# Sample attention woven into prompt attention, ahead of the delta rule

## The reference

```
n = RMSNorm(x);  [A | B] = n @ w_in
h = x + w_out @ concat(A, B);   y = h + PEER(RMSNorm(h))
A: softmax attention, 8 heads x 64, dilated windows (128,1), (512,4), (2048,16)
   sample: 4 queries x 8 heads against 2048 cached keys/values per sequence
B: gated delta rule, 4 heads, key and value width 128
PEER: 16384 single-neuron experts, 8 product-key heads, top 16
outputs: y_prompt, y_sample, K/V windows, conv and delta states of both groups
```

## Time and profile before

| | us |
|---|---|
| median of 3 runs (lowest, highest) | 2330.55 (2328.76, 2334.92) |
| the profiled execution's time | 2327.75 |
| its span, first to last instruction | 2325.8 |
| PE busy | 2071.7 (89%) |
| DVE busy | 1576.0 (68%) |
| POOL busy | 1153.3 (50%) |
| ACT busy | 775.6 (33%) |
| mean granted clock of PE, share of full speed | 0.938 |

### The profile page before, as it was taken

The page is one execution under the profiler, slowest core; times in us unless marked ns, Lnnn a source line. Parts: engine busy times, 40 slices in busy tenths (PEclk is TensorE's granted clock), DMA queues, the critical chain, the costliest instruction groups (busy, mean ns, idle before and its releaser), DMA issues.

```text
span 2325.8 us, 34649 instructions
## 1 busy us (share of the span) xinstructions
PE 2071.7 (89%) x12706; PEld 1919.7 (83%) x12706; DVE 1576.0 (68%) x3094; ACT 775.6 (33%) x1230; POOL 1153.3 (50%) x632
## 2 busy tenths in 40 slices
PE   5999998787567898999999788889989999999998
PEld 5989756675346898999888788879979999999998
DVE  2378434433332301879986999994369999999996
ACT  3223233222232322444444434333323333333332
POOL 2326002131001231566676344337778888888884
PEclk9999758896798899999999999999989999999999
DMA  6453245542874121467777667678978989899894
GB/s 220 145 176 115 73 192 215 217 152 79 277 253 137 53 88 60 140 213 239 227 237 243 223 241 273 231 279 340 355 281 313 331 310 317 309 314 315 316 324 138
DMA packets 176596, 520.94 MB, mean 224 GB/s; under 512 B 15152, under 2 KB 86064, under 8 KB 170704
## 3 DMA queue, kind: packets, MB, share of 16 engines
q1 hardware_dynamic: 136560, 290.94, 36.2%
q0 software_dynamic: 36864, 134.23, 17.2%
q10 hardware_dynamic: 3056, 94.24, 10.3%
HBM read 456.81 MB, written 128.49 MB: 252 GB/s over the span
## 4 chain that ended last, share of the span: by engine, by line
PE 42%; DVE 40%; issue 6%; ACT 4%; POOL 3%; DMA 3%; SPq 2%; ACTq 0%; DVEq 0%; PEldq 0%
DVE acc_g L1850 10%; DVE act_l L1834 9%; PE bank L2210 7%; PE bank L2211 6%; PE bank L2212 6%; DVE one L1529 6%; DVE one L1528 5%; DVE rows_g L1698 3%; PE twin L2210 3%; PE twin L2212 3%; PE twin L2211 3%; POOL u_lo L1673 2%; PE bank L464 1%; DMA ks<-kc 1%; PE bank L646 1%
## 5 line engine op out<-in xcount | busy, mean ns | idle before, releaser
L1673 POOL TENSOR_TENSOR u_lo<-u_raw,u_hi 128x1024 fp32r<-128x1024 f32 x128 | 315.9, 2468 | 330.1 <-ACT u_hi L1653 329.4
L2210 PE MATMUL bank<-hn_hi,u_hi 128*128 128x416 f32 x1024 | 373.8, 365 | 33.9 <-POOL u_lo L1673 33.6
L1878 POOL TENSOR_TENSOR v_lo<-v_raw,v_hi 128x1024 fp32r<-128x1024 f32 x128 | 336.0, 2626 | 70.4 <-ACT v_hi L1803 69.2
L2211 PE MATMUL bank<-hn_lo,u_hi 128*128 128x416 f32 x1024 | 363.6, 355 | 0.0
L2212 PE MATMUL bank<-hn_hi,u_lo 128*128 128x416 f32 x1024 | 362.0, 354 | 0.0
L1850 DVE SCALAR_TENSOR_TENSOR acc_g<-rows_g,coef,acc_g 128x1024 f32<-128x1024 f32 x127 | 289.3, 2278 | 18.0 <-DMA rows_g<-ev,idx_g 17.6
L2211 PE MATMUL bank<-a_lo,v_hi 128*128 128x416 f32 x768 | 269.4, 351 | 0.0
L2210 PE MATMUL bank<-a_hi,v_hi 128*128 128x416 f32 x768 | 269.2, 351 | 0.0
L2212 PE MATMUL bank<-a_hi,v_lo 128*128 128x416 f32 x768 | 269.1, 350 | 0.0
L2210 PEld LDWEIGHTS bank<-hn_hi,u_hi 128*128 128x128 f32 x1024 | 195.9, 191 | 49.2 <-POOL u_lo L1673 47.1
L1834 DVE TENSOR_TENSOR act_l<-act_l,gin 128x416 f32<-128x416 f32 x128 | 229.6, 1794 | 0.0
(11 more groups left out here) (436 smaller groups left out, 4740.8 us busy)
## 6 DMA issues: line engine op xcount, KB each, us to landing
u_raw<-eu SPq DMA_DIRECT2D x128, 512.0 KB, 4.9
v_raw<-ev SPq DMA_DIRECT2D x128, 512.0 KB, 4.7
k_s<-kc ACTq DMA_DIRECT2D x29, 1104.0 KB
v_s<-vc ACTq DMA_DIRECT2D x29, 1104.0 KB
acts_dram<-act_c SPq DMA_DIRECT2D x128, 208.0 KB, 3.8
gates_dram<-gst ACTq DMA_DIRECT2D x8, 3328.0 KB, 12.5
gin<-gates_dram SPq DMA_DIRECT2D x32, 832.0 KB, 7.9
act_l<-acts_dram SPq DMA_DIRECT2D x64, 416.0 KB, 5.6
```

Source lines behind the costliest of these rows:

```text
L1673: nc.gpsimd.tensor_tensor(out=u_lo[s][:], in0=u_raw[2 * (x % 2) + s][:], in1=u_hi[s][:].bitcast(F32), op=ALU.subtract).then_inc(dn["ulo"], 1)
L1878: nc.gpsimd.tensor_tensor(out=v_lo[f % 4][:], in0=v_raw[f % 4][:], in1=v_hi[f % 4][:].bitcast(F32), op=ALU.subtract).then_inc(dn["vlo"], 1)
L2210: nc.tensor.matmul(out, ah, bh, start=first and i == 0, stop=False)
L2211: nc.tensor.matmul(out, ah, bl, start=False, stop=False)
```

## The change

The sample stage is dissolved into prompt attention. Each sample batch has four consecutive slots (`SLOTS_B`), one prompt unit each. PE turns key pairs 0 and 1 around unit 0, pairs 2 and 3 around unit 1, turns the previous batch's probabilities ahead of unit 2 and computes the batch's scores after it, and multiplies the previous batch's values ahead of unit 3. The PSUM banks are shared: prompt scores have two banks and run two units ahead, turned prompt probabilities one bank, prompt values one, and the sample work the other four. K, V, `kt_lo`, `kt_hi` and `qbd` go to the space of the projection's input and weights, which is free when the last projection product is out, and SP issues their first loads then. The queries' block matrix `qbd` is written by DVE ahead of the first scores. The delta rule starts when both attentions are done. The delta states are loaded after the last values; the first w_out slice has a buffer of its own (`w_first`) and is loaded then too. Its split by ACT comes after the delta rule's last copy, and POOL's low halves wait for the store of the sample states, whose space `w_lo` shares. The copies of the cache are 10 pairs in the projection (slices 2 to 11), none in attention, 12 in the delta rule, 8 in the query products.

The diff, cut to its core:

```diff
         ks = [put(f"ks{s}", [P, KTILES, AH * AD]) for s in range(2)]
-        vs_old = [None, put("vs_old1", [P, OLD_TILES, AH * AD])]
-        assert put.pos[0] <= R_W
-        put = region(R_AQ)
-        vs_old[0] = put("vs_old0", [P, OLD_TILES, AH * AD])
-        vs_new = [put(f"vs_new{s}", [P, NEW_TILES, AH * AD]) for s in range(2)]
-        assert put.pos[0] <= R_AV
-        kt_lo = at("kt_lo", R_BZ, [P, PAIRS, KT_SPLIT])
-        put = region(R_E)
+        vs = [put(f"vs{s}", [P, KTILES, AH * AD]) for s in range(2)]
+        kt_lo = put("kt_lo", [P, PAIRS, KT_SPLIT])
+        kt_hi = put("kt_hi", [P, PAIRS, CACHED - KT_SPLIT])
+        qbd = put("qbd", [P, NB, PAIRS, QROWS])
+        assert put.pos[0] <= R_AQ
+        put = region(R_E + 8192 + 4096)
         sss = [put(f"sss{s}", [P, CACHED + QROWS]) for s in range(2)]
         pts = put("pts", [P, KTILES + 1, QROWS])
-        qbd = put("qbd", [P, NB, PAIRS, QROWS])
-        kt_hi = put("kt_hi", [P, PAIRS, CACHED - KT_SPLIT])
+        put = region(R_STAT + 160)
         ob = put("ob", [P, P])
         seat_t = put("seat_t", [P, P + PAIRS * NL])
         own_half, fold = seat_t[:, 0:P], seat_t[:, P:]
+        assert put.pos[0] <= R_STAT + 160 + NT * 64 + 3 * CH * 32
+        w_first = at("w_first", R_E, [P, CH, WC])
...
-        COPIES_W, COPIES_A, COPIES_D = NW1 // 2, -(-SEQ // P * AH // 3), 2 * (LEVELS - 1)
-        COPIES = COPIES_W + COPIES_A + COPIES_D
+        COPIES_W, COPIES_D, COPIES_F = 10, 2 * (LEVELS - 1), 8
+        COPIES = COPIES_W + COPIES_D + COPIES_F
...
+        TURN_LO, TURN_HI, SCORE_LO, SCORE_HI = 4, 5, 6, 7
+        value_out = bank[TURN_LO][:, 0:P]
+        folded = bank[SCORE_LO][:, 0:PAIRS * NL]
...
+        def sp_attend(sp):
+            sp.wait_ge(proj_ready, READY1)
+            sp.wait_ge(w_lo_ready, NW1)
+            for b in range(2):
+                load_cached(sp, b, kc)
+            sp.wait_ge(rope_done, NT)
+            sp.dma_start(seat_t[:], lnc_s[:, CACHED + NB * QROWS:]).then_inc(small_in, 16)
+            for b in range(2):
+                load_cached(sp, b, vc)
+            for b in range(2, NB + 1):
+                if b < NB:
+                    sp.wait_ge(sa["kt0"], PAIRS * (b - 1))
+                    sp.wait_ge(sa["kt1"], PAIRS * (b - 1))
+                    load_cached(sp, b, kc)
+                if b > 2:
+                    sp.wait_ge(sa["used"], b - 2)
+                    load_cached(sp, b - 1, vc)
+            sp.wait_ge(sa["used"], NB)
+            sp.wait_ge(s_cat, len(UNITS) // 2)
+            sp.dma_start(w_first[:], wout[0]).then_inc(w_in[0], 16)
+            sp.dma_start(w_raw[1][:], wout[1]).then_inc(w_in[1], 16)
...
             def scores(u):
                 i, h = UNITS[u]
-                if u >= 4:
-                    pe.wait_ge(s_masked, u - 3)
+                if u >= 2:
+                    pe.wait_ge(s_masked, u - 1)
                 r = slice(AD * (h % 2), AD * (h % 2) + AD)
-                nc.tensor.matmul(bank[2 + u % 4][:, 0:(i + 1) * P], qkt[r, h // 2, i * P:(i + 1) * P],
+                nc.tensor.matmul(bank[2 + u % 2][:, 0:(i + 1) * P], qkt[r, h // 2, i * P:(i + 1) * P],
                                  qkt[r, PAIRS + h // 2, 0:(i + 1) * P], start=True, stop=True).then_inc(s_scores, 1)
 
             def turn(u):
                 i, h = UNITS[u]
                 pe.wait_ge(s_norm, u + 1)
-                if u >= 2:
-                    pe.wait_ge(s_pt, u - 1)
+                if u:
+                    pe.wait_ge(s_pt, u)
                 for j in range(i + 1):
-                    last = nc.tensor.transpose(quad(u % 2)[:, j, :], sm[:, u % 4, j * P:(j + 1) * P], ident)
+                    last = nc.tensor.transpose(quad(0)[:, j, :], sm[:, u % 4, j * P:(j + 1) * P], ident)
                 last.then_inc(s_turned, 1)
...
+            def turn_keys(b, p):
+                s, q = b % 2, b * PAIRS + p
+                if p == 0:
+                    pe.wait_ge(keys_in[s], 16 * 4 * (b // 2 + 1))
+                    if b >= 2:
+                        pe.wait_ge(s_kept, KEPT0 + b - 1)
+                if q:
+                    pe.wait_ge(sa["kta"], q)
...
+            def sample_scores(b):
+                pe.wait_ge(sa["kta"], PAIRS * (b + 1))
+                pe.wait_ge(sa["ktv"], PAIRS * (b + 1))
+                if b:
+                    pe.wait_ge(sa["masked"], b)
+                if b >= 2:
+                    pe.wait_ge(sa["os"], b - 1)
...
+            def turn_sample(b):
+                s = b % 2
+                pe.wait_ge(sa["norm"], b + 1)
+                keys_turned = PAIRS * min(b + 2, NB)
+                pe.wait_ge(sa["kta"], keys_turned)
+                pe.wait_ge(sa["ktv"], keys_turned)
+                if b == NB - 1:
+                    pe.wait_ge(s_kept, KEPT0 + b)
...
+            def fold_heads(b):
+                pe.wait_ge(small_in, 16 * 10)
+                pe.wait_ge(s_kept, KEPT0 + b + 1)
+                pe.wait_ge(sa["masked"], min(b + 2, NB))
+                if b == NB - 1:
+                    pe.wait_ge(sa["os"], b)
+                nc.tensor.matmul(folded, ob[:], fold, start=True, stop=True).then_inc(s_fold, 1)
+
+            pe.wait_ge(sa["q"], 1)
+            scores(0)
+            scores(1)
             for u in range(len(UNITS)):
+                b, k = divmod(u, SLOTS_B)
+                if k == 0:
+                    if b >= 2:
+                        fold_heads(b - 2)
+                    turn_keys(b, 0)
+                elif k == 1:
+                    turn_keys(b, 2)
+                elif k == 2 and b:
+                    turn_sample(b - 1)
+                elif k == 3 and b:
+                    sample_values(b - 1)
                 turn(u)
                 if u:
                     values(u - 1)
-                if u + 4 < len(UNITS):
-                    scores(u + 4)
+                if u + 2 < len(UNITS):
+                    scores(u + 2)
+                if k == 0:
+                    turn_keys(b, 1)
+                elif k == 1:
+                    turn_keys(b, 3)
+                elif k == 2:
+                    sample_scores(b)
             values(len(UNITS) - 1)
+            fold_heads(NB - 2)
+            turn_sample(NB - 1)
+            sample_values(NB - 1)
+            fold_heads(NB - 1)
...
+            dve.wait_ge(proj_ready, READY1)
+            chain.link(nc.vector.memset(qbd[:], 0.0))
+            for h in range(AH):
+                r = slice(AD * (h % 2), AD * (h % 2) + AD)
+                chain.mark(nc.vector.tensor_copy(qbd[r, :, h // 2, (h % 2) * NL:(h % 2 + 1) * NL],
+                                                 qkt[r, h // 2, SEQ:TOK].rearrange("p (b l) -> p b l", b=NB)))
+            chain.join()
+            dve.sem_inc(sa["q"], 1)
...
             mask(0)
-            mask(1)
             for u in range(len(UNITS)):
-                if u + 2 < len(UNITS):
-                    mask(u + 2)
+                b, k = divmod(u, SLOTS_B)
+                if k in (1, 2):
+                    keys(b, 2 * k - 1)
+                if u + 1 < len(UNITS):
+                    mask(u + 1)
+                if k in (0, 1):
+                    keys(b, 2 * k)
                 n = (UNITS[u][0] + 1) * P
                 dve.wait_ge(s_exp, u + 1)
                 chain.link(nc.vector.reciprocal(smax[:, u % 4, 3:4], smax[:, u % 4, 2:3]))
                 nc.vector.tensor_scalar(sm[:, u % 4, 0:n], sm[:, u % 4, 0:n], smax[:, u % 4, 3:4], None, ALU.mult).then_inc(s_norm, 1)
+                if k == 1 and b:
+                    sample_norm(b - 1)
+                if k == 3:
+                    sample_mask(b)
+                    if b:
+                        own_heads(b - 1)
+            sample_norm(NB - 1)
+            own_heads(NB - 1)
...
             exponentials(0)
-            exponentials(1)
             for u in range(len(UNITS)):
-                if u + 2 < len(UNITS):
-                    exponentials(u + 2)
-                if u % 3 == 0:
-                    copy_cache(act, COPIES_W + u // 3)
+                b, k = divmod(u, SLOTS_B)
+                if k in (1, 2):
+                    keys(b, 2 * k - 1)
+                if u >= 3 and u % 2:
+                    pair(u // 2 - 1)
                 if u:
                     turned(u - 1)
-                if u >= 3 and u % 2:
-                    pair(u // 2 - 1)
+                if k == 0 and b >= 2:
+                    keep_heads(b - 2)
+                if k in (0, 1):
+                    keys(b, 2 * k)
+                if u + 1 < len(UNITS):
+                    exponentials(u + 1)
+                if k == 0 and b:
+                    sample_exp(b - 1)
+                if k == 2 and b:
+                    sample_turned(b - 1)
             turned(len(UNITS) - 1)
             pair(len(UNITS) // 2 - 1)
+            keep_heads(NB - 2)
+            sample_exp(NB - 1)
+            sample_turned(NB - 1)
+            keep_heads(NB - 1)
...
```

(27 more changed lines are left out.)

308 lines of the change are left out of this document (114 added, 194 removed).

## The result

The changed kernel took 2307.14 us in the median of 12 runs (2295.6 to 2316.41), the kernel before 2329.22 in 12 on the same chip: a ratio of 0.991, 95% interval 0.9891 to 0.9929. It is faster by 22 us, under 1% but clear of the interval; 45 were forecast. The profiled execution took 2308.13 us with a span of 2306.3, against the 2280.3 of the sum. The 26 us between these two are the subject here.

The account below looks back on a forecast made before the run. Serial prompt and sample attention were taken as the cost, at low clock and hand-over waits: 2325.8 - 98.2 - 138.3 + 180 + 11 = 2280.3 us of span, 2285 as measured time; own range 2255 to 2310, over all cases 2255 to 2338.

Parts of the forecast that it names:

- The walk of the woven stage: Slot-by-slot sum of PE's work and waits in the merged attention: 173 us at 2.4 GHz, 277 at 1.2 GHz.
- I take x = 0.1: Share of the woven stage assumed at 1.2 GHz, a tenth; it turns 173 us into 173/(1 - 0.038) = 180.
- no gap above 1.3 us: Woven stage: PE never idles longer than this, one reason given for taking the high clock level.
- Rival 2: Woven stage: mixed clock (204 us at 40% low, 214 at 50%) or little overlap (206); time 2309 to 2318, chance 0.13.
- Rival 1: Whole woven stage: clock stays low, 277 us instead of 180, time 2382; chance 0.15.
- Copies. Taken as 0, bound +5: Moving cache copies out of attention into projection and query products costs 0 us, bounds -1 to +5.
- The slack of 20 us a slice: Weight splits: POOL waits 265 us over 12 slices, so POOL and raw buffers can absorb copies issued ahead.
- The output products' start: First output product comes 11 us (6.5 to 44.5) after the delta rule's last write, through states' store and POOL's low half.
- Loads of keys and values: Woven stage: issued seven to eight slots ahead, cost 0; without that cover 28.7 us of waits return.
- Query blocks: Ahead of the first scores: a memset and eight copies of the queries, 2.65 us.
- Delta rule: Its time stays within 5 us of before.
- all from the query products on: Everything from the query products to the kernel's end stays within 5 us of before.

Follow-up runs that it names:

- run 4: Changed kernel plus unread TensorE products ahead of the first scores and in slots 0 and 1 of each batch: 0.983 of the kernel before, 2288.18 us.
- run 8: Changed kernel plus unread TensorE products in slots 0 and 1 alone, none ahead of the first scores: 0.985 of the kernel before.
- run 10: Changed kernel with eight copy pairs woven, first slice split early, query blocks early, unread products in slots 0 and 1 and at the start: 0.9761, 2268.77 us.
- run 1: The changed kernel again, no edit: 0.9889 of the kernel before, 2300.03 us.
- run 12: Changed kernel plus four unread TensorE products ahead of the first scores alone: 0.9903 of the kernel before.
- run 6: Kernel before, unwoven, plus unread TensorE products in the prompt attention alone: 0.9999 of the kernel before.
- run 9: Changed kernel with the first output-weight slice split early into its own buffers, during the delta rule's last group: 0.9866 of the kernel before.
- run 13: Changed kernel with four of the eight copy pairs in the query products at twice the distance, four in the woven stage: 0.9893 of the kernel before.

## Why the prediction was right or wrong

- **The walk of the woven stage was right, the clock's share was not.** The step that failed is "I take x = 0.1". The trace shows 26%, and with that the prediction's own formula gives 173/(1 - 0.38 x 0.26) = 192 us, against 190.3. With the clock held (run 4) the stage is 172.5. The reason given, that there was "no gap above 1.3 us", was no reason: the clock fell with no wait above 1.4 us before it, in 342 and 391, and unread products put where the 17 waits for the scaling stood removed the falls in the middle of the stage in three profiles (runs 4, 8 and 10). The waits were forecast to the tenth and costed only as waits. That they alone cause the falls is not shown: the same 20.7 us of them went with mean clocks of 0.83, 0.87 and 0.92 (run 1, the first profile, run 12), and in run 6 the clock rose by products added where PE did not wait.
- **Rival 2 was the nearest.** It is the mixed clock, 204 us at 40% low; the stage had 26%. Rival 1, low throughout, did not come, since the clock rose again each time, in 355 to 360 with a batch's values running (88 instructions in 5 us). The Trainium skill, "TensorE: Matmul & The Clock Gate", Part 4, read as the prediction reads it, would have had the stage low throughout, for its transposes; the trace does not agree: the upper level holds for three quarters of it.
- **"Copies. Taken as 0, bound +5" failed.** They cost 7 us behind skt_s (12 in two profiles) and under 1 to 3 in the query products; moved alone in the kernel before, in pairs a tenth larger, 22. The slack of 20 us a slice was misread: the 265 us of rows 8 hold two waits of 92.7 and 63.1 us ahead of the first two slices; in the query products of the kernel before POOL mostly waited 8.0 us a slice:

```profile
876.40 4.59 POOL L1540 TENSOR_TENSOR w_lo<-w_raw,w_hi 128x2048 fp32r<-128x2048 f32 x1 [8.01 <-ACT w_hi L1162]
```

  And the working never asked how long a pair holds the DMA engines (12 us, every 12.6) nor what is loaded right after the last one. The woven stage (10.3) and what follows skt_s (7.7) make up 18 us of the 26.
- **The output products' start was right**: 9.8 us against 11, by the named chain of store and POOL's low half, with errors of about 1 us that partly cancel (store 8.75 us against 10, low half 5.45 against 4.6). The output products themselves then took 3.1 us longer than before, which was not foreseen; the last section tells why.
- **Loads of keys and values, right**: no wait. Query blocks, 2.65 us: 2.9. Delta rule, within 5 us: 1.5. That "all from the query products on" would stay "within 5 us of before" failed: it took 11.1 us more.
- The direction was right for the reason given: 98.2 + 138.3 us became 190.3 + 9.8. The time, 2307, lies inside the stated 2255 to 2310, near its slow end; of the gain of 45 us, half came.

## What to carry to other kernels

When work is woven to fill an engine's idle time, price the clock along with the slots: a stage with short waits every few us can lose more through the clock than by the waits' length, and here unread products in them won back 18 of 190 us of the stage (12 of the kernel's time). Before a background transfer is moved, divide its bytes by the rate that it gets alone and compare with the time between issues; a queue that never drains falls due at the first load that someone waits for. And what an operation took beside a busy neighbour is not what it takes when the order changes.

## What was not expected of the hardware

DVE and POOL stop each other. The four parts of cat_lo on DVE, the same operation, in the kernel after; parts one and two lie in the first row, three and four in the others:

```profile
689.80 2.49 DVE L1441 TENSOR_TENSOR cat_lo<-cat,cat_hi 128x1088 fp32r<-128x1088 f32 x2 [3.83 <-ACT cat_hi L1353]
```

```profile
692.21 5.60 DVE L1441 TENSOR_TENSOR cat_lo<-cat,cat_hi 128x1088 fp32r<-128x1088 f32 x1
```

```profile
697.74 5.66 DVE L1441 TENSOR_TENSOR cat_lo<-cat,cat_hi 128x1088 fp32r<-128x1088 f32 x1
```

The first two take 2.49 us together; the others 5.6 each, about as long as POOL's subtraction beside them (5.45 and 5.62 us, at 691.21 and 696.63), which itself takes 4.6 us when DVE is quiet. In run 9 POOL comes later and the four parts take 4.90 us together, 8.7 less. The Trainium skill, "SBUF — State Buffer", section "SBUF: two separate sides", says that a DVE operation with two inputs from SBUF and a GpSimd one that reads SBUF exclude each other for a whole instruction; the trace agrees: each slow part ends 1.15 us after the subtraction beside it, nearly its own length (1.28 us alone).

This is also why the output products took longer. SP loads the inputs X only when all four parts of cat_lo are out, here at 703.42; DVE's first sum, which frees a PSUM bank, waits for them until 712.71, and PE for DVE:

```profile
713.19 0.39 PE L2241 MATMUL twin<-w_hi,cat_hi 128*128 128x256 f32 x1 [2.95 <-DVE X L1450]
```

Then the clock is at 0.50 in 715 to 717. Such a wait of 2.5 to 3.9 us stands in all ten profiles in which parts three and four of cat_lo took 5.6 us, and in none of runs 9 and 10 and the kernel before, where all four took 1.28 each. In run 9 the first product comes 7.2 us earlier and the output products take 65.2 us instead of 69.0, together the 11.

A pair of DRAM-to-DRAM copies moved 188 GB/s in run 13 with no load asked for beside it, at a busy share of the DMA engines of 0.43 to 0.70; the stretch with loads of keys and the states' store under way reached 372.
